# Delta rule: halves, products and turns of the inverse levels put between the contraction steps of the projection tiles

## What is computed

```python
proj = h @ w_in                                   # the projection: 32 tiles of 128 features
qkv = silu(causal_dwconv(qkv, conv_w))            # 24 of the tiles: k, q, v (4 taps)
m = where(strict, einsum(k_beta, k) * decay, 0)   # per chunk and head
a_mat = eye + m
u = triangular_solve(a_mat, v_beta, lower=True)
w = triangular_solve(a_mat, k_beta * exp(g), lower=True)
...
v_new = u_i - w_i @ state; o_i = q_i @ state + qk_i @ v_new; state = state * a + k_i @ v_new
```

## Time and profile before

| | |
|---|---|
| median of 3 runs | 1244.25 us (1243.69 to 1245.8) |
| span of the profiled execution | 1243.2 us |
| PE busy | 1223.5 us, 98% |
| DVE busy | 736.0 us, 59% |
| ACT busy | 722.2 us, 58% |
| POOL busy | 880.3 us, 71% |
| mean granted TensorE clock | 0.993 |

### The profile page before, as it was taken

How to read it: one execution, slowest core, us unless ns; L and a number is a source line. 1 busy time by engine, 2 the same in 40 slices (tenths; PEclk the granted TensorE clock), 3 DMA queues, 4 the chain that set the end, 5 groups by cost and what they waited for, 6 DMA issues and landing times.

```text
span 1243.2 us, 26081 instructions
## 1 busy us (share of the span) xinstructions
PE 1223.5 (98%) x9026; PEld 1127.9 (91%) x9026; DVE 736.0 (59%) x1718; ACT 722.2 (58%) x1325; POOL 880.3 (71%) x387
## 2 busy tenths in 40 slices
PE   9999999999999999999999999999999999999997
PEld 3678899988998888889999999999999999999986
DVE  3989972244587774159884375555634757555633
ACT  3656654565666665479642366666655547666753
POOL 0357857568869888957533248888898868888795
PEclk9999999999999999999998999999999999999999
DMA  9995355446646665645332126555566555656562
GB/s 369 408 366 186 102 187 153 119 149 205 183 142 210 190 186 164 188 146 162 118 98 75 52 88 190 182 183 172 159 187 196 174 166 170 193 180 185 154 200 71
DMA packets 66038, 217.76 MB, mean 175 GB/s; under 512 B 9904, under 2 KB 17328, under 8 KB 62624
## 3 DMA queue, kind: packets, MB, share of 16 engines
q1 hardware_dynamic: 65952, 216.59, 55.0%
HBM read 215.52 MB, written 1.05 MB: 174 GB/s over the span
## 4 chain that ended last, share of the span: by engine, by line
issue 38%; POOL 37%; PE 22%; ACT 1%; POOLq 1%; DVE 1%; ACTq 0%; DVEq 0%
POOL w_lo L673 36%; PE bank L802 10%; PE bank L1135 5%; PE bank L894 3%; PE bank L903 1%; PE bank L898 1%; POOL w_lo L680 1%; POOLq L670 0%; ACT h L1689 0%; ACT w_hi L1689 0%; POOLq L672 0%; PE bank L948 0%; PE bank L724 0%; PE bank L729 0%; PE bank L725 0%
## 5 line engine op out<-in xcount | busy, mean ns | idle before, releaser
L673 POOL TENSOR_TENSOR w_lo<-w_raw,w_hi 128x1024 fp32r<-128x1024 f32 x340 | 812.8, 2404 | 325.1 <-ACT w_hi L1689 323.7
L1689 ACT ACTIVATE w_hi<-w_raw 128x1024 fp32r<-128x1024 f32 (+1 forms) x372 | 378.1, 1020 | 103.0 <-PE bank L903 34.8
L802 PE MATMUL bank<-a_hi,w_hi 128*128 128x264 f32 (+3 forms) x704 | 200.5, 285 | 0.6 <-DVE a_lo L3670 0.6
L802 PE MATMUL bank<-a_hi,w_lo 128*128 128x264 f32 (+3 forms) x704 | 200.2, 284 | 0.0
L802 PE MATMUL bank<-a_lo,w_hi 128*128 128x264 f32 (+3 forms) x704 | 199.9, 284 | 0.0
L802 PEld LDWEIGHTS bank<-a_hi,w_hi 128*128 128x128 f32 x704 | 132.9, 189 | 0.8 <-DVE a_lo L3670 0.8
L802 PEld LDWEIGHTS bank<-a_lo,w_hi 128*128 128x128 f32 x704 | 132.9, 189 | 0.1
L802 PEld LDWEIGHTS bank<-a_hi,w_lo 128*128 128x128 f32 x704 | 132.9, 189 | 0.0
L3745 DVE SCALAR_TENSOR_TENSOR bank<-row_mean,cols,bank 128x260 f32<-128x260 f32 (+3 forms) x112 | 54.6, 488 | 115.8 <-ACT cols L1689 113.0
L763 PE MATMUL bank<-a_parts,w_hi 128*128 128x256 f32 x448 | 81.5, 284 | 0.5 <-DVE a_parts L2952 0.4
L894 PE MATMUL bank<-g_parts,w_hi 128*128 128x512 f32 x308 | 78.9, 396 | 0.0
(11 more groups left out here) (548 smaller groups left out, 2933.1 us busy)
## 6 DMA issues: line engine op xcount, KB each, us to landing
w_raw<-in_s SPq DMA_DIRECT2D x284, 512.0 KB, 3.6
w_raw<-in_down SPq DMA_DIRECT2D x48, 512.0 KB, 3.5
adaw<-in_w_ada SPq DMA_DIRECT2D x16, 1024.0 KB, 9.7
w_raw<-in_down SPq DMA_DIRECT2D x24, 384.0 KB, 3.3
adab<-in_w_ada_first SPq DMA_DIRECT2D x8, 1024.0 KB, 8.7
ctxt<-in_ctx SPq DMA_DIRECT2D x1, 1024.0 KB, 11.3
x<-in_x SPq DMA_DIRECT2D x1, 1024.0 KB, 15.3
out_h<-h SPq DMA_DIRECT2D x4, 256.0 KB, 2.6
```

Source lines behind the costliest of these rows:

```text
L673: pool.tensor_tensor(w_lo[:, s], w_raw[:, s], w_hi[:, s].bitcast(F32), ALU.subtract) \
L802: ins = mm(banks[bank][:, tk], w_[:, s, k], x_[:, k, tk], start=(m == 0), stop=(m == 3 * KD - 1))
L1689: return nc.scalar.activation(out_, in_, f, **kw)
```

## The change

A new function, `a_in_beside(t, beside)`, issues one tile of the projection like `a_in`, but calls `beside(k)` after each contraction step k, and the small work is issued there. `y` can be issued in two parts of four heads. Nothing is added to or taken from the computation, and the order on ACT, DVE, POOL and SP is as before.

- Tile 19: four half heads of level 4's `y` after steps 4 to 7 (before: both `y` after the tile). Tile 22 the same for level 5.
- Tile 20: `ty(1)`, `ty(2)`, `turned(1)`, `turned(2)` of level 4 after steps 4 to 7 (before: after the tile). Tile 23 the same for level 5.
- Tile 24: `y(1, 6)` and `y(2, 6)` after steps 6 and 7; `by_token("kt0")` now stands before tile 24 and not after it.
- Tile 25: `new_values(0)`, `ty(1, 6)`, `ty(2, 6)` after steps 5, 6, 7. Tile 26: `turned(1, 6)` after step 2, `turned(2, 6)` after step 4.

```diff
--- before.py
+++ after.py
@@ -1307,6 +1307,20 @@
             def a_in(first, last):
                 lin("a_in", N2, whole2, tiles=(first, last), first=Z0 if first >= 24 else 0)
 
+            def a_in_beside(t, beside):
+
+
+                pe.wait_ge(lo_ready, UNIT0["a_in"] + t + 1)
+                pe.wait_ge(banks_free, TILE0["a_in"] + t + 1)
+                n0 = Z0 if t >= 24 else 0
+                for k in range(KD):
+                    for m, (w_, x_) in enumerate(((w_hi, whole2[0]), (w_hi, whole2[1]), (w_lo, whole2[0]))):
+                        ins = mm(banks[t % SLOTS][:, n0:N2], w_[:, t % SLOTS, k], x_[:, k, n0:N2], start=(k == 0 and m == 0),
+                                 stop=(k == KD - 1 and m == 2))
+                    if k == KD - 1:
+                        ins.then_inc(unit_used, 1)
+                    beside(k)
+
             def head_rows(name, src, n0, n1, m):
 
                 claim(name)
@@ -1395,16 +1409,19 @@
                         ins = mm(dst, pick16[:, k], diag16[:, :, k + 1:], start=True, stop=True)
                     ins.then_inc(stage_done, 1)
 
-            def y(c, lv):
+            HEADS = range(HN)
+
+            def y(c, lv, part=HEADS):
 
                 cn, B, name = CHUNKS[c][1], cb[c], f"y{c}.{lv}"
 
-                read_out(f"ty{c}.{lv - 1}" if lv > FIRST else f"fI{c}")
-                if lv == FIRST:
-                    pe.wait_ge(mt_ready, 2 * c)
-                claim(name)
+                if part.start == 0:
+                    read_out(f"ty{c}.{lv - 1}" if lv > FIRST else f"fI{c}")
+                    if lv == FIRST:
+                        pe.wait_ge(mt_ready, 2 * c)
+                    claim(name)
                 b = BANKS[name][0]
-                for hh in range(HN):
+                for hh in part:
                     if lv == LOG2P - 1:
                         ins = mm(in_rows(b, HALVES[1], GC)[:, hh], B["mt"][0:GC, hh, GC:], B["tt"][0:GC, hh, 0:GC],
                                  start=True, stop=True)
@@ -1416,7 +1433,8 @@
                         for first, second in QUARTERS:
                             ins = mm(in_rows(b, second, 32)[:, hh], B["mt"][first, hh, second], B["tt"][first, hh, first],
                                      start=True, stop=True)
-                ins.then_inc(stage_done, 1)
+                if part.stop == HN:
+                    ins.then_inc(stage_done, 1)
 
             def ty(c, lv):
 
@@ -1577,10 +1595,19 @@
             flip("fI2", 2, "uu")
             products("kq1", 1, qr)
             products("kq2", 2, qr)
-            a_in(19, 20)
-
-            y(1, 4)
-            y(2, 4)
+            def first_halves(k):
+                if k >= 4:
+                    y(1 + (k - 4) // 2, 4, (HEADS[0:4], HEADS[4:8])[k % 2])
+
+            def products_and_turns(lv, k0):
+
+                def beside(k):
+                    if k >= k0:
+                        (ty, ty, turned, turned)[k - k0](1 + (k - k0) % 2, lv)
+
+                return beside
+
+            a_in_beside(19, first_halves)
             claim("ckq")
             pe.wait_ge(klen_ready, 1)
             token_rows(5, (7,))
@@ -1588,39 +1615,41 @@
                 ins = mm(banks[5][0:CN0, P + hh * CN0:P + (hh + 1) * CN0], kr[:, hh, 0:CN0], qr[:, hh, 0:CN0],
                          start=True, stop=True)
             ins.then_inc(stage_done, 1)
-            a_in(20, 21)
-            ty(1, 4)
-            ty(2, 4)
-            turned(1, 4)
-            turned(2, 4)
+            a_in_beside(20, products_and_turns(4, 4))
             a_in(21, 22)
             by_token("kt1", 1, kr)
             by_token("kt2", 2, kr)
-            a_in(22, 23)
-
-            y(1, 5)
-            y(2, 5)
+
+            def second_halves(k):
+                if k >= 4:
+                    y(1 + (k - 4) // 2, 5, (HEADS[0:4], HEADS[4:8])[k % 2])
+
+            a_in_beside(22, second_halves)
             decay_of_queries(1)
             decay_of_queries(2)
-            a_in(23, 24)
-            ty(1, 5)
-            ty(2, 5)
-            turned(1, 5)
-            turned(2, 5)
-            a_in(24, 25)
+            a_in_beside(23, products_and_turns(5, 4))
             by_token("kt0", 0, kr)
 
-            y(1, 6)
-            y(2, 6)
+            def last_halves(k):
+                if k >= 6:
+                    y(k - 5, 6)
+
+            a_in_beside(24, last_halves)
             pe.wait_ge(conv4_act, 24)
             by_token("vt0", 0, vr)
-            a_in(25, 26)
-            new_values(0)
-            ty(1, 6)
-            ty(2, 6)
-            turned(1, 6)
-            turned(2, 6)
-            a_in(26, 27)
+
+            def first_values(k):
+                if k == 5:
+                    new_values(0)
+                elif k > 5:
+                    ty(k - 5, 6)
+
+            def last_turns(k):
+                if k in (2, 4):
+                    turned(k // 2, 6)
+
+            a_in_beside(25, first_values)
+            a_in_beside(26, last_turns)
 
             state_update(0)
             by_token("vt1", 1, vr)
```

## The result

The changed kernel takes 1249.92 us in the median of 11 runs (1248.15 to 1259.63), the kernel before 1245.23 in 11 runs of the same comparison (1242.5 to 1247.29): 1.0068 times as long, with a 95% interval of 1.0048 to 1.0087. That is slower, as forecast, and the median lies at the forecast's 1249.6, but this agreement is luck and hides what happened.

- six at 1248.15 to 1249.92 us, mean 1248.7, with a mean granted clock of 0.997;
- five at 1257.0 to 1259.63 us, mean 1258.5, with 0.988 or 0.989.

The account below looks back on a forecast made before the run. PE, busy for 98% of the span, was taken to set the pace. Terms 4.3 - 0.8 + 2.2 + 1.0 - 1.35 = +5.35 us on a 1243.2 span, plus 1.05 to the median, gave 1249.6 us; range 1245.2 to 1251.6.

Parts of the forecast that it names:

- Term 1: Tiles 19 to 26 on PE: 16 new returns to the tile at 0.29 us, less four seams: +4.3 us.
- rival of free borders: The 16 borders in the tiles cost nothing: 1245.3 us with one clock fall, 1243.6 with none; chance 0.12.
- Term 2: PE's waits for DVE go: 0.24 us before level 4's second turn, 0.56 before level 5's first; -0.8 us.
- Term 3: Before `kt0`, PE newly waits for DVE's copies out of two banks, tile 24's cover being gone: +2.2 us.
- Term 4: Level 5 follows DVE's chain: PE waits 0.9 to 1.0 us before `ty(1, 5)` and `turned(1, 5)`; +1.0 us.
- Term 5: Clock: level 6's old fall gone or shorter, -3.05 us; one new 3.4 us fall from the stalls, +1.7 us.
- rival of no fall: The clock does not fall at all in the new stage: 1247.9 us; chance 0.22.
- the forecast of one: One clock fall in the new stage, net -1.35 us for the clock: 1249.6 us; chance 0.40.
- The rule on transposes: Transposes don't count as busy for the clock like other matmuls; a fall after `kt0` likelier, not in the sum.

Follow-up runs that it names:

- e9: The changed kernel with level 6's turns after steps 0 and 1 of tile 26 instead of 2 and 4; 1253.39 us, 1.0077 of the kernel before.
- e8: The kernel before with only `new_values(0)` (16 rows) put inside tile 25, after step 3; 1242.93 us, 0.9988 of the kernel before.
- e1: The changed kernel with `kt0` issued after step 5 of tile 24 instead of ahead of the tile; 1255.15 us, 1.0083 of the kernel before.
- e3: The kernel before with only the change in tiles 25 and 26 (level 6's new values, products and turns); 1252.45 us, 1.007 of the kernel before.
- e4: The kernel before with only the half heads of `y` put into tiles 19 and 22; 1246.69 us, 1.0014 of the kernel before.
- e7: The kernel before with only `ty` and `turned` of levels 4 and 5 put into tiles 20 and 23; 1244.39 us, 1.0000 of the kernel before.
- e2: The changed kernel with the change kept only in tiles 19 to 24, tiles 25 and 26 as before; 1251.0 us, 1.0045 of the kernel before.
- e5: The changed kernel with both turns of level 6 moved behind a whole tile 26; 1251.0 us, 1.0049 of the kernel before.
- e12: The changed kernel with level 6's turns after steps 0 and 1 of tile 26, run once more for a trace; one run of 1254.26 us.
- e11: The kernel before with `new_values(0)` and level 6's `ty` inside tile 25, turns ahead of a whole tile 26; 1246.74 us, 1.0016 of the kernel before.

## Why the prediction was right and wrong

**Term 1, borders: right.** Tile 19 in the changed kernel's timeline of PE:

```profile
626.28 0.29 PE L1318 MATMUL bank<-a_lo,w_hi 128*128 128x272 f32 x1
626.41 0.29 PE L1318 MATMUL bank<-a_hi,w_lo 128*128 128x272 f32 x1
626.62 0.66 PE L1430 MATMUL bank<-tt,mt 64*64 64x32 f32 x16
627.21 0.39 PE L1318 MATMUL bank<-a_hi,w_hi 128*128 128x272 f32 x1
627.44 0.29 PE L1318 MATMUL bank<-a_lo,w_hi 128*128 128x272 f32 x1
```

0.21 us in, and 0.23 between the first and second large matmul, as predicted from the borders of the earlier trace rows. In total: the stage lasted 53.2 us before with its fall taken out (55.91 less 2.7, the worth of that fall, below) and lasts 59.4 now (63.67 less the 4.3 that its fall cost, from e9's trace), +6.2. Idle time of PE is 1.6 of that: 3.05 us, less 1.18 and less the 0.31 that PE would have waited before too at full clock (e8). That leaves 4.6 for borders, 0.29 for each of 16, where I had 0.29 each and 4.3 in all. The rival of free borders has fallen. By the rule of the Trainium skill, page TensorEngine Tiling (Array Packing), section Tiling Modes, that a change of mode drains TensorE, every border pays; the trace agrees, with 0.21 us here against 0.13 between two large matmuls.

**Term 2: right.** Neither the 0.24 nor the 0.56 is there in its old form.

**Term 3, the wait before `kt0`: right,** 2.1 us with the second bank, where I had 2.2. DVE and ACT in the changed kernel's timeline, to be set against X, the start of tile 23's last matmul (655.75):

```profile
656.07 0.49 ACT L1718 ACTIVATE vr<-bank,pv 128x272 f32<-128x272 f32 x1 [5.95 <-PE bank L1318]
...
656.59 1.57 DVE L3183 SCALAR_TENSOR_TENSOR vr<-bank,pv,vr 128x269 f32<-128x269 f32 x3 [1.26 <-ACT vr L1718]
658.08 1.28 DVE L3296 COPY uu<-bank 128x512 f32<-128x512 f32 x2
```

The first copy is done at 658.72, X + 3.0, as worked out, and `kt0` starts at 658.81 after 1.9 us; its 8 records take 1.20 and not 1.03, which is the wait for the second bank. e1 gets this back: its stage takes 57.1 us (618.62 to 675.75, at full clock), 2.3 less than the 59.4.

**Term 4: right,** 0.25 and 0.64 us in place of 0.56, together 0.9 where I had said 0.9 to 1.0 in one place or two.

**Terms 1 to 4 together** came to +6.7; measured +6.2 in the stage at full clock, and +5.6 over the whole run between runs with a mean clock of 0.997. The parts add up: level 6's part +0.7 (e3, 53.87 us for the stage, without a fall in it), half heads +2.2 (e4, 57.13 less 1.7 for its 3.4 us fall), products and turns +0.7 (e7, 56.57 less 2.7 for its 6.8 us fall), `kt0`'s wait 2.3 (e1). That is 5.9, and the cut in tile 24, which none of these kernels has alone, is some 0.3 more.

**Term 5, the clock: this is the step that failed.** It stood at -3.05 + 1.7: with 21 large matmuls spread between `new_values(0)` and the last turn the fall of the earlier trace rows was to be gone or shorter, and one fall of 3.4 us at the stall was to take its place. The first half is what failed. In 5 of 11 runs the clock is lost far longer than before. In the profiled one it falls in level 6, later by some work but behind the same kind of work, and stays down for 17.1 us and not 6.8; with the second late fall that makes 23.9 us at 0.50 in three falls, and the group stands 10 us above the other.

In the other six runs the term may have held. They stand at 1248.7, between the rival of no fall (1247.9, with a chance of 0.22) and the forecast of one (1249.6), their mean clock is that of traces with one fall of 3.4 us, and e9's trace, at 1248.38, has that fall in tile 23 and none in level 6. It cost 1.1 us there and not 1.7, since PE would have waited for part of that time. But `kt0`'s stall did not start it: it began 3.9 us before PE stood still for `kt0`, behind the smaller wait of term 4. The other four traces with both waits (the changed kernel, e2, e5, e12) have no fall at that place, and e1 keeps the upper group without the stall.

The rule on transposes that I had drawn on beside this (the Trainium skill, TensorE: Matmul & The Clock Gate, Part 4) made a fall behind `kt0` likelier. No trace has one behind `kt0`: in the changed kernel the clock stayed at 1.00 through the turns of level 5, 1.9 us of standstill and `kt0`'s transposes, and in e9 it was back by then. e9's fall has level 5's turns in it, which are transposes too, so that the rule is neither borne out nor refuted here.

The value that I gave to the old fall, 3.05 us, was also too high: e8 at full clock waits 0.31 for DVE at the second turn, so 2.7.

I had reasoned from the mean share of large matmuls over the stage. What seems to decide is what stands close together: `ty(1, 6)` comes three large matmuls behind the 16-row group, and behind the fall come tile 26 in pieces and then `state_update(0)`, whose 16 records of 16 rows take 3.78 us where they took 2.05. The changed kernel's timeline of PE there:

```profile
682.47 3.78 PE L1511 MATMUL bank<-vb,kdc 16*128 16x128 f32 x16
686.17 1.97 PE L1365 MATMUL bank<-ident,vr 128*128 128x128 f32 x8
```

At half clock the small work lasts nearly twice as long and so parts the large work further, so that a fall may hold itself. This mechanism is argued and not shown, from e12 and e11, whose falls end earlier with more large matmuls in a row; the state update was not moved, so its own share was not tried. What e2 and e3 show is only the place: tiles 25 and 26.

**What stays open.** Why the clock falls in some runs of one kernel and not in others; why e5's and e9's upper runs lie in two heights each; whether the lower group of the changed kernel has the fall that e9's trace shows; and whether the late fall at 733.8 follows from the earlier ones. The three traces whose fall in level 6 lasted 10.2 us or more (the changed kernel, e11, e12) have two late falls each, and none of the others has more than one.

## What to carry to other kernels

Putting small-corner matmuls between the steps of a large tile costs about 0.3 us for each cut and wins only the wait that it covers; here there was 0.8 us to win, and a dependent step that lost its cover (`kt0`) took back 2.1. If small work must be spread for the clock's sake, move the few-row group alone, far from the next one, and leave the tile that follows whole (e8: 0.9988, a gain that the interval just separates from none). Look at the single runs and their granted clocks before a median is believed: a change can have two times, and the median names one of them.

## What the runs showed of the hardware

- With PE busy in all of its records, the granted clock fell to 0.50 behind groups of 16 and 64 rows that stood close together, and in the changed kernel it stayed there for 17.1 us; in the same trace a standstill of 1.9 us amid transposes of full rows brought no fall.
- Whether it falls differs between runs of one kernel on the same chip: 1248.15 and 1259.63 us.
- What a fall costs depends on what else would have waited: 10.2 us at 0.50 with PE busy throughout cost 4.3 us (changed kernel against e9), and 3.4 us just ahead of a wait for DVE cost 1.1 (e9).
- Putting a small-corner group between two steps of a large tile cost 0.29 us each time (4.6 us for 16).
- With one group of 16 matmuls placed after tile 25's step 3 in place of behind the tile, the mean clock was 0.9965 over 12 runs against 0.9940 over 23 of the kernel before, and the time 0.9988 of it.
